# Three sums of squares as two rounded products each, and one more step of a value block before the first scores

## What is computed

```python
k = rms_norm(k.reshape(b, s, N_HEADS, HEAD_DIM), k_norm_g)
q = rms_norm((h @ q_w).reshape(b, s, N_HEADS, HEAD_DIM), q_norm_g)
# rms_norm: x * rsqrt(mean(x*x, axis=-1) + EPS) * g
logits = q @ k * scale + (F[t] - F[s])       # causal
out = softmax(logits) @ v                    # then @ o_w, added to the stream
```

## Time and profile before

| | before |
|---|---|
| median of 3 runs | 1198.12 us |
| profiled execution | 1198.92 us |
| its span | 1197.1 us |
| TensorE (PE) busy | 1179.0 us, 98% |
| VectorE (DVE) busy | 763.2 us, 64% |
| ScalarE (ACT) busy | 499.5 us, 42% |
| GpSimd (POOL) busy | 24.4 us, 2% |
| share of TensorE in the chain that ended last | 90% |
| sums of squares as one product (L915) | 4, in 8 records of 590 ns |
| sums of squares as two (L918, L920) | 12, each product 389 ns |

### The profile page before, as it was taken

The page is one execution under the profiler, slowest core; times in us unless marked ns, Lnnn a source line. Parts: engine busy times, 40 slices in busy tenths (PEclk is TensorE's granted clock), DMA queues, the critical chain, the costliest instruction groups (busy, mean ns, idle before and its releaser), DMA issues.

```text
span 1197.1 us, 17104 instructions
## 1 busy us (share of the span) xinstructions
PE 1179.0 (98%) x5899; PEld 989.9 (83%) x5899; DVE 763.2 (64%) x1119; ACT 499.5 (42%) x815; POOL 24.4 (2%) x37
## 2 busy tenths in 40 slices
PE   6999999999999999999999999999999999999998
PEld 4788889888888888889978888889888888888887
DVE  5656888875665665555979898986743443443442
ACT  5422332542332332333767778864531331331431
POOL 2000000000000000002010000000000000000000
PEclk9999999999999999999999999999999999999999
DMA  9767654576666565332355544441333333333333
GB/s 335 230 194 245 189 177 132 156 237 192 187 206 196 174 200 166 88 91 71 89 141 136 130 107 124 122 127 52 90 90 103 90 104 89 104 91 101 91 102 89
DMA packets 228642, 168.77 MB, mean 141 GB/s; under 512 B 5636, under 2 KB 210604, under 8 KB 228588
## 3 DMA queue, kind: packets, MB, share of 16 engines
q1 hardware_dynamic: 228396, 167.92, 48.0%
q0 software_dynamic: 32, 0.07, 0.0%
q10 hardware_dynamic: 160, 0.06, 0.0%
HBM read 153.24 MB, written 2.10 MB: 130 GB/s over the span
## 4 chain that ended last, share of the span: by engine, by line
PE 90%; DVE 6%; ACT 1%; issue 1%; SPq 1%; DMA 1%; DVEq 0%; ACTq 0%
PE bank L609 28%; PE bank L611 28%; PE bank L610 28%; PE bank L956 1%; PE bank L974 1%; PE bank L707 1%; PE bank L946 1%; DVE w_lo L1543 1%; DMA first_raw<-in_sc_w_in 1%; PE bank L947 1%; DVE neg_max L2022 1%; SPq L385 1%; PE bank L737 0%; DVE h_lo L1592 0%; DVE probs L2035 0%
## 5 line engine op out<-in xcount | busy, mean ns | idle before, releaser
L609 PE MATMUL bank<-h_hi,w_hi 128*128 128x512 f32 (+1 forms) x864 | 326.2, 378 | 2.0 <-issue 1.1
L611 PE MATMUL bank<-h_hi,w_lo 128*128 128x512 f32 (+1 forms) x864 | 322.7, 373 | 0.0
L610 PE MATMUL bank<-h_lo,w_hi 128*128 128x512 f32 (+1 forms) x864 | 322.6, 373 | 0.0
L1117 ACT ACTIVATE w_hi<-raw 128x1024 fp32r<-128x1024 f32 x184 | 193.3, 1054 | 259.6 <-DMA raw<-in_mlp_w 222.3
L609 PE MATMUL bank<-g_hi,w_hi 128*128 128x512 f32 (+1 forms) x696 | 261.8, 376 | 0.0
L611 PE MATMUL bank<-g_hi,w_lo 128*128 128x512 f32 (+1 forms) x696 | 259.2, 372 | 0.0
L610 PE MATMUL bank<-g_lo,w_hi 128*128 128x512 f32 (+1 forms) x696 | 259.0, 372 | 0.0
L1543 DVE TENSOR_TENSOR w_lo<-raw,w_hi 128x1024 fp32r<-128x1024 f32 x184 | 224.7, 1224 | 45.7 <-ACT w_hi L1117 42.7
L609 PEld LDWEIGHTS bank<-h_hi,w_hi 128*128 128x128 f32 x864 | 162.6, 188 | 32.7 <-issue 3.2
L610 PEld LDWEIGHTS bank<-h_lo,w_hi 128*128 128x128 f32 x864 | 162.7, 188 | 28.7 <-issue 0.5
L611 PEld LDWEIGHTS bank<-h_hi,w_lo 128*128 128x128 f32 x864 | 162.6, 188 | 28.8
(11 more groups left out here) (225 smaller groups left out, 1072.1 us busy)
## 6 DMA issues: line engine op xcount, KB each, us to landing
raw<-in_mlp_w SPq DMA_DIRECT2D x128, 512.0 KB, 4.1
ada_raw<-in_ada_w SPq DMA_DIRECT2D x40, 1024.0 KB, 5.6
raw<-in_sc_w_in SPq DMA_DIRECT2D x20, 512.0 KB, 4.4
ada_first<-in_ada_w SPq DMA_DIRECT2D x32, 256.0 KB, 7.9
raw<-in_w_kv SPq DMA_DIRECT2D x16, 512.0 KB, 3.9
raw<-in_sc_w_out SPq DMA_DIRECT2D x8, 512.0 KB, 3.9
raw<-in_q_w SPq DMA_DIRECT2D x8, 512.0 KB, 4.7
keys<-qk SPq DMA_DIRECT2D x16, 256.0 KB, 3.1
```

Of the source, the lines that this page charges most:

```text
L609: mm(out[:, cols], weights_hi, hi[:, k, cols], start=(k == 0), stop=False)
L610: mm(out[:, cols], weights_hi, lo[:, k, cols], start=False, stop=False)
L611: return mm(out[:, cols], weights_lo, hi[:, k, cols], start=False, stop=(k == KT - 1))
L1117: go(w_hi[:, jj, :, :], raw[:, jj, :, :], ACT.Copy).then_inc(hi_ok, 1)
```

## The change

k0, k1 and q1 leave `WHOLE_SQUARES`; of the four only q0 stays. ScalarE gets three copies, VectorE three subtractions (for k0 between the query tiles, for k1 behind `low("k", 0)`, for q1 behind `head_norm("k", 1)`), TensorE six products in place of three. k0's high part gets a place of its own, the first half of `tb`, since `sq_hi`'s is in use then; `v_copy(0)`, which writes there, waits for k0's sum. k0's sum moves behind the last two half steps of v0. On ScalarE `v_high(0)` moves ahead of q0's square. TensorE makes one more step of v1 ahead of the first scores, and from there to the sum of k2 the steps of k2 and q2 are each placed one earlier or one later, so that the total is the same. SyncE issues the copies of q's high part once that is ready, and waits for the low part only before its copy, for every pair. For the last pair ScalarE makes all four exponentials of head 13 ahead of rounding q7.

```diff
-WHOLE_SQUARES = (("k", 0), ("q", 0), ("k", 1), ("q", 1))
+WHOLE_SQUARES = (("q", 0),)
...
+    first_sq_hi, = stacked(region_tb, [("first_sq_hi", [P, T], F32R)])
...
+    def high_square(kind, j):
+        return first_sq_hi[:] if (kind, j) == ("k", 0) else sq_hi[:]
...
             def head_queries(j, half):
...
-                sp.wait_ge(q_ok, j + 1)
+                sp.wait_ge(q_hi_ok, j + 1)
                 if j:
                     sp.wait_ge(s_ok, TT * (h - 1))
                 copy(queries[own, :, half, :], qk[own, 0:1, 0, :].broadcast_to([HD, 2, T])).then_inc(queries_in[half], 16)
+                sp.wait_ge(q_ok, j + 1)
                 copy(queries[other, 0, half, :], qk[own, 1, 0, :]).then_inc(queries_in[half], 16)
...
-                    mm(out, ones_head[:], sq_hi[:], start=True, stop=False)
+                    mm(out, ones_head[:], high_square(kind, j), start=True, stop=False)
...
-            kvq("v", 0, range(0, 6), cols=HALF[1])
+            kvq("v", 0, range(KT), cols=HALF[1])
             head_sum("k", 0)
-            kvq("v", 0, range(6, KT), cols=HALF[1])
...
             head_sum("q", 1)
-            kvq("v", 1, range(3, 4))
+            kvq("v", 1, range(3, 5))
...
             logits(0)
-            kvq("v", 1, range(4, KT))
-            kvq("k", 2, range(0, 2))
+            kvq("v", 1, range(5, KT))
+            kvq("k", 2, range(0, 3))
             turn_probs(0)
-            kvq("k", 2, range(2, 5))
+            kvq("k", 2, range(3, 6))
             logits(1)
...
-            kvq("k", 2, range(5, KT))
+            kvq("k", 2, range(6, KT))
             pe.wait_ge(v_copied, 2)
-            kvq("q", 2, range(0, 2))
+            kvq("q", 2, range(0, 3))
             turn_probs(1)
-            kvq("q", 2, range(2, 5))
+            kvq("q", 2, range(3, 5))
             pe.wait_ge(hn_read, NORM_OF["q", 1] + 1)
             head_sum("k", 2)
...
                 if (kind, j) not in WHOLE_SQUARES:
                     act.wait_ge(hn_sq, SQUARE_OF[kind, j] + 1)
-                    act.wait_ge(hn_pe, NORM_OF[kind, j])
-                    go(sq_hi[:], tb[:, SQUARE_SLOT[kind, j], :], ACT.Copy).then_inc(hn_hi, 1)
+                    if (kind, j) != ("k", 0):
+                        act.wait_ge(hn_pe, NORM_OF[kind, j] if (kind, j) != ("k", 1) else NORM_OF["k", 0] + 1)
+                    go(high_square(kind, j), tb[:, SQUARE_SLOT[kind, j], :], ACT.Copy).then_inc(hn_hi, 1)
...
-                if j == 1:
-                    act.wait_ge(hn_pe, NORM_OF["q", 0] + 1)
+                if j < 2:
+                    act.wait_ge(hn_pe, NORM_OF["kq"[j], 0] + 1)
...
             after_block("k", 1)
+            v_high(0)
             head_square("q", 0)
-            v_high(0)
             head_root("q", 0)
...
-                exponentials(2 * i + 1, 0, 2)
+                exponentials(2 * i + 1, 0, 2 if nxt < KT - 1 else TT)
                 high("q", nxt)
-                exponentials(2 * i + 1, 2, TT)
+                if nxt < KT - 1:
+                    exponentials(2 * i + 1, 2, TT)
...
             query_tile(3)
+            square_low("k", 0)
             query_low(2)
...
             low("k", 0)
+            square_low("k", 1)
             v_low(0)
             after_block("k", 1)
             head_norm("q", 0)
             low("q", 0)
             head_norm("k", 1)
+            square_low("q", 1)
             after_block("q", 0)
             after_block("q", 1)
             maxima(0)
```

More of the change, by code:

```diff
@@ L2001, in square_low @@
                 dve.wait_ge(hn_hi, PARTS_OF[kind, j] + 1)
-                tt(sq_lo[:], tb[:, 1, :], sq_hi[:], ALU.subtract).then_inc(hn_lo, 1)
+                tt(sq_lo[:], tb[:, 1, :], high_square(kind, j), ALU.subtract).then_inc(hn_lo, 1)
             def low(kind, j):
```

## The result

The changed kernel takes 1201.38 us (median of 12 runs, 1200.33 to 1202.42) against 1198.24 us (12 runs): a ratio of 1.0024 with a 95% interval of 1.0017 to 1.0032. It is slower by 2 to 4 us. The time lies in the predicted range, above the predicted 1200.3. It is also above the line of 0.2% that the prediction drew: it gave 0.37 to that side and 0.60 to a time within the line. The profiled execution took 1200.98 us, where 1201.1 was predicted for it.

What follows compares the result with a forecast made beforehand. VectorE's order of work was taken to set the time from head 1's scores to head 3's turn (656.05). First scores 2.27 us late, taken as +2.2 on 1198.12, gave 1200.3 us, range 1198.9 to 1202.2.

Steps and rivals of the forecast that it cites:

- The products' cost: TensorE's sums of squares: two rounded products take 0.41 us less than a whole one, 1.23 us for three.
- ScalarE's and VectorE's 0.65: At k0: each rounded square's copy costs ScalarE 0.65 us, and VectorE's split moves 0.65 too.
- q0: q0's square on ScalarE starts 0.42 us later, its sum about 0.41 later, with a stall of about 1.0.
- q1, the step that decides: q1's low half, behind k1's norm on VectorE, is ready at 616.40; TensorE's next v1 step is 1.89 us late.
- First scores and head 1's: Both sets of scores 2.27 us late; one more v1 step adds 0.68, the queries' 0.30 wait goes.
- VectorE's chain: From head 1's scores to head 3's turn VectorE's order sets the time, unchanged at 30.33 us from head 1's maxima.
- B: Rival: part of VectorE's chain is TensorE's, so the moved step and 0.38 stall count: +1.2, 1199.3 us; chance 0.12.
- Priced at nothing: Last pair's exponentials ahead of q's rounding, earlier query copies of pairs 1 to 7, k0's own slot: no cost or gain.
- The sum: Whole kernel: +2.27 us, taken as +2.2 because small slacks tend to give a tenth back.
- Rival A, the clock: TensorE's gaps at q0's and q1's sums bring the slow clock, 1.72 us lost: 1202.0 us; chance 0.08.
- C: Rival: the products' saving carries, q1's low half being there by 614: 1196.6 us; chance 0.03.
- D: Rival: q1's waits as priced but everything else hides, 0 to +0.5, about 1198.5 us; chance 0.05.

Runs made afterwards that it cites:

- k0 alone: Changed kernel with only k0's sum in two rounded products, k1 and q1 whole, v's rounding and steps as before, early query copies kept: ratio 0.9997.
- the fourteenth: Only k0's sum in two products, plus one k2 step moved from before head 1's scores to behind head 0's output: ratio 0.9997.
- the experiment: Changed kernel with SyncE waiting for q's low part before both copies again and head 13's exponentials split around q7's rounding: ratio 1.0023.
- two of its variants: Changed kernel with v1's extra step back behind the first scores, 1.0016; changed kernel with VectorE's first weight split ahead of q1's subtraction, 1.0034.
- the six kernels with both waits: Changed kernel, its rerun, and four variants that keep TensorE's waits before q1's high and low products: ratios 1.0016 to 1.0034.

## Why the prediction came out as it did

*The products' cost, ScalarE's and VectorE's 0.65, k0, q0, k1:* right. q0's sum was forecast 0.41 later in absolute time and is 0.43 later in the count from k0's square.

*q1, the step that decides:* right. The low product was to start 616.45 - 613.93 = 2.52 us later than the whole one had; it starts 27.10 - 24.54 = 2.56 later.

*First scores and head 1's:* forecast 2.27 late, in the traces 2.33 and 2.31. The queries' wait at the first scores is gone, because TensorE comes later: with the early copies taken back the scores stand where they are, and with k0 alone most of the wait is still there.

*VectorE's chain:* right for this change. From head 1's scores to head 3's turn it is 31.07 to 31.09 us in thirteen of the fourteen profiles, whether eight steps or nine stand between head 1's and head 2's scores, and though the clock was low in front of it in two. B would have it vary by 0.68. In the fourteenth it is 31.35: ten steps stand there, and the moved one makes k2's block late. So "the chain is VectorE's" holds only while k2's block ends in time. A detail was wrong: the step taken out returns first as a wait at head 2's scores, for VectorE's low probabilities (637.29, 0.44 us later than the cadence), then 0.13 at head 2's turn and 0.51 at head 3's. I had named only the turns.

*Priced at nothing:* right, by the experiment.

*The sum:* +2.27 against 2.33 at head 13's turn. The tenth I took off for slack, to +2.2, was not there.

*Rival A, the clock:* this is where the text failed. I priced it at 1.72 us from the kernel's start; it measured 1.57 and 1.56. Its sign, a granted clock under 1.00, is not in the changed kernel's two profiles and is in those of two of its variants. But I treated it as something that either happens to the kernel or doesn't, with 0.08. By the mean clocks it happens in some executions and not in others of the same program, so it belongs in the median and the range of the forecast itself. The loss by the ratio exceeds the trace's own 2.3 us by 0.6 (1.0024) and 0.4 us (1.0023). A single such excess says nothing, with intervals of about 1 us to either side, but all thirteen kernels can be set against their traces: the loss by the ratio, less the loss at head 13's turn (with the 1.57 and 1.56 taken out of the two profiles at low clock). In the six kernels with both waits the excess is 0.25 to 0.61 us, 0.4 on average; in the seven others it is -0.39 to 0.18, -0.1 on average. Together with the mean clocks above, this makes the clock's share in the median well supported. How often it falls stays open; two of six profiles at 1.56 us would give 0.5 us (an estimate). That it falls there, and what it costs, two profiles show.

*C and D:* no low half came early, and nothing hid the delay.

*Between the two sides:* the prediction thought a loss under 0.2% likelier. The 2.33 us of the trace alone are 0.19%, so it is the excess that brings the ratio over the line, and the interval, 1.0017 to 1.0032, holds both sides of it.

## What to carry to other kernels

Before a cheaper form of an operation is taken, find where its extra input is made in the other engine's order: here 1.2 us of products were to be saved, and q1's sum, whose one subtraction stands behind a dependent norm, cost 1.5. A saving on a saturated engine is real only up to the next wait that other engines set, so save what lies in front of such a wait with slack on the makers (k0), not what lies behind it (k1, q1). When a wait can't be avoided, put independent work in front of it on the waiting engine: reordering alone gave back 1.4 of 2.3 us here.

## What was not expected of the hardware

**A wait can cost more than its length, in some executions only.** In two of the six profiles of kernels with both waits, TensorE was busy for 1.56 of 3.60 us and for 1.25 of 4.40 us, and then had half the clock until 619 and until about 621, at about 1.56 us each. The changed kernel's own two profiles have the same waits (0.91 and 1.12 us, 0.88 and 1.14) and a granted clock of 1.00 behind them. The Trainium skill, "TensorE: Matmul & The Clock Gate", Part 1, says that the clock falls to half after the engine has been idle; the traces agree that it falls after waits, though TensorE had a product between its two and was never idle for more than 1.13 us in the first instance. Why it falls in one execution and not in the next, no run here shows.

**The same clock makes the start uneven.** The kernel before had 0.79 and 0.86 between 19.5 and 30 us. The windows of k0 alone at the start:

```profile
19.00:23.00 4.00, 3.46 (x17) 1.31 (x17) 3.57 (x7) 2.05 (x4) 0.00 (x0) 1.00 1.09 361
23.00:30.00 7.00, 7.00 (x38) 5.86 (x38) 5.75 (x11) 2.99 (x4) 0.00 (x0) 1.00 1.09 355
```

It started k0's square at 587.52 us, the kernel before at 589.39, and the span of 1194.8 us is mostly that, not the edit. A single span says little about half a microsecond; places counted from an event in front of the edit repeat to 0.04 us.

**GpSimd and VectorE in each other's way.** GpSimd's timeline in the changed kernel:

```profile
603.79 1.48 POOL L603 TENSOR_TENSOR fg_u<-fg_f,neg_f 16x512 f32<-16x512 f32 x1
```

The same instruction took 1.16 us before, and VectorE's subtraction for k1, beside it at 603.35, took 0.90 instead of 0.68. Both were off the path. The Trainium skill, "SBUF — State Buffer", in the section on its two sides, says that a VectorE instruction with two inputs in SBUF and a GpSimd instruction that reads SBUF share a pair of ports as an exclusive lock; the traces agree in that both got longer, and don't show that one was kept out for the whole length of the other.
